# A decoder trunk on one core: the first pair of up blocks fed with unnormalised h, the reciprocal root and shift applied to its result

## The chip, the cores and the metric

One core of one Trainium2 chip runs the whole program in one launch. The metric is the device time in microseconds (us), the median of several executions. A profile is one further execution, recorded by the hardware profiler; its times are counted from the start of its span.

## What is computed

Four layers, each a token mixer (short convolution, RWKV-7, gated linear attention, short convolution) and then a gated convolutional FFN. There are 512 prompt tokens and 8 sample tokens, D = 1024 and 2816 hidden columns. The part that the change touches is the normalisation between the mixer and the FFN, and the first two hidden tiles:

```python
h = h + gt_m * rmsnorm(out, p['norm_g'][l, 1])
u = rmsnorm(h, p['norm_g'][l, 2]) * (1 + sc_f) + sh_f
# conv_ffn:
h_gate, h_val = jnp.split(x @ w_up, 2, axis=-1)
hc, new_buf = causal_dwconv(h_gate, buf, conv_w)
out = (jax.nn.silu(hc + conv_b) * h_val) @ w_down
```

`rmsnorm(x, g)` is `x * rsqrt(mean(x*x) + eps) * g`, with the mean over the 1024 columns of a token. sc_f, sh_f and gt_m come from the conditioning vector, one set for the prompt and one for each sample token. The root is one number for each token, so (h * a * r + s) @ W equals r * ((h * a) @ W) + s @ W, where a is the gain times (1 + sc_f), r the reciprocal root and s the shift.

## The kernel before

**Layout.** Activations lie transposed: 128 columns on the partitions, k = 0..7 tiles, and T = 520 tokens along the free axis (512 prompt, then 8 samples). h, proj (the output of the previous GEMM), u_hi and u_lo have this form. A GEMM operand is split into a high part, rounded to fp32r, and the low remainder.

**Blocks.** A block is one 128-column output of a GEMM. For each weight block SyncE loads w_raw (two slots, by parity), ScalarE rounds it to w_hi (`high`, 128x1024), GpSimd writes w_raw - w_hi to w_lo (`low`; `low_parts` does the same in four pieces of 128x256), and TensorE runs three products, hi x hi, lo x hi and hi x lo, each in two halves of 260 tokens: 48 matmuls of 260 columns. A load waits until the low part of the block two before it is done (`load_block`). The up GEMM has 22 hidden tiles of two blocks each, the gate block (even, PSUM pair 0) and the value block (odd, PSUM pair 1).

**Norms.** After the last block of "out" comes the plan's step "post": sums of squares of proj over the tokens (`token_sums`, TensorE), square root (`root`, ScalarE), reciprocal (`inverse_root`, VectorE), a spread of the reciprocal over all partitions into PSUM (`spread_rstd`, TensorE), and then on VectorE for each tile k a multiplication of proj by it (`times_rstd`) and the update of h. Then comes "pre" for the FFN: ScalarE squares each tile of h, TensorE sums, root, reciprocal and spread follow again, VectorE writes h times the reciprocal to `normed`, ScalarE makes u_hi and the unrounded u (`usb`) from it with scale and shift, and VectorE makes u_lo. TensorE's `gemm_pair` starts with the first tile of u: it runs blocks n0 and n0+1 tile by tile, 12 matmuls for each k, as the tiles come.

**Fill.** In layers 0 to 2 TensorE also does in the two norms the 16 modulation products of the next half layer (`ada_ahead`, four matmuls for each of them), in fixed places: four before post's spread, four behind it, four between the sums of pre, four behind pre's spread. Layer 3 has none. Every engine runs its instructions in the order written; the waits on semaphores are written by hand.

**Start of up.** For each hidden tile ScalarE copies the state columns (`place_state`) and the gate block into `gate`, frees PSUM pair 0, and rounds the next tile's first weight block; VectorE runs a convolution of three steps (`conv3`); ScalarE applies Silu and rounds the next tile's second weight block; VectorE multiplies by the value block (`times_tile`, which frees PSUM pair 1) and splits the product (`split_hidden`). TensorE transposes the tile's last rows (`turn_tail`) and the next state (`turn_state`) between tiles.

## Time and profile before

| | |
|---|---|
| runs | 3015.1, 3015.58 and 3020.77 us, median 3015.58 us |
| span of the profiled execution | 3014.3 us |
| TensorE matmuls | 2876.1 us, 95% of the span |
| VectorE | 1528.4 us, 51% |
| GpSimd | 1321.5 us, 44% |
| ScalarE | 1085.0 us, 36% |
| all that TensorE sat idle for ScalarE's squares (L1717 <- L1011) | 25.2 us |
| chain that ended last, TensorE's share | 62% |

The profiled execution stands 1.3 us under the median of the runs. Engines are PE = TensorE, DVE = VectorE, ACT = ScalarE, POOL = GpSimd, SP = SyncE. In a timeline, a row gives start, duration, engine, line of the kernel, operation, operands and count; what ended an idle time before it stands in brackets. A timeline row of two or more instructions has the time from the first's start to the last's end; an fp32 matmul counts as two records, an fp32r one as one.

### The profile page before, as it was taken

What the parts mean: (1) busy time and instruction counts of PE and PEld (TensorE: products, weight loads), DVE (VectorE), ACT (ScalarE), POOL (GpSimd) and SP (SyncE); (2) the same over time, 40 slices, a digit from 0 to 9 for tenths busy, and PEclk for the clock granted to TensorE, in tenths of its full rate; (3) what the DMA queues carried; (4) which work ended last, traced back from release to release, by engine and by line L of the source; (5) the groups of instructions that cost most, each with busy time, mean ns of one, the idle gap of its engine ahead of it and who ended that gap; (6) DMA issues with size and microseconds to landing.
All of it is one profiled execution on the core that took longest, in us unless ns stands there. A gap on an engine that the chain in (4) does not pass through costs nothing.

```text
span 3014.3 us, 72962 instructions
## 1 busy us (share of the span) xinstructions
PE 2876.1 (95%) x29617; PEld 2733.3 (91%) x29617; DVE 1528.4 (51%) x2080; ACT 1085.0 (36%) x2139; POOL 1321.5 (44%) x959
## 2 busy tenths in 40 slices
PE   6999999998989999999998999999999999899998
PEld 5998999997978877899997899889999899799998
DVE  3435666118357874666603242476650444566612
ACT  4224333225455652433323444343332422433322
POOL 3443444442435554344443273434444344344443
PEclk9999999999999999999999999999999999899999
DMA  7544333544411013333354323533334543133332
GB/s 269 164 151 159 95 92 88 158 128 136 119 44 32 4 37 124 120 89 92 99 159 152 99 64 112 169 123 89 92 116 146 173 120 91 57 92 92 91 91 85
DMA packets 465618, 332.56 MB, mean 110 GB/s; under 512 B 19914, under 2 KB 435608, under 8 KB 465122
## 3 DMA queue, kind: packets, MB, share of 16 engines
q1 hardware_dynamic: 461400, 325.24, 35.1%
q10 hardware_dynamic: 4010, 4.22, 0.6%
q8 instruction: 172, 2.82, 0.4%
q14 instruction: 36, 0.29, 0.0%
HBM read 319.62 MB, written 10.20 MB: 109 GB/s over the span
## 4 chain that ended last, share of the span: by engine, by line
PE 62%; DVE 4%; ACT 2%; issue 1%; DMA 1%; SPq 0%; POOL 0%; ACTq 0%; DVEq 0%
PE banks L1667 33%; PE banks L1675 16%; PE banks L2126 5%; PE banks L2133 1%; PE banks L1628 1%; PE banks L1973 1%; DVE h L2662 1%; PE banks L1690 1%; DVE proj L2606 1%; PE banks L1761 0%; DMA s_state<-in_state_wkv_b_dram 0%; ACT conv L1080 0%; PE banks L2135 0%; ACT uv L1433 0%; DVE proj_b L2606 0%
## 5 line engine op out<-in xcount | busy, mean ns | idle before, releaser
L765 POOL TENSOR_TENSOR w_lo<-w_raw,w_hi 128x1024 fp32r<-128x1024 f32 x395 | 1007.5, 2551 | 1108.1 <-ACT w_hi L981 1088.0
L1667 PE MATMUL banks<-u_hi,w_hi 128*128 128x260 f32 x4064 | 834.5, 287 | 14.2 <-ACT w_hi L981 9.4
L1667 PE MATMUL banks<-u_lo,w_hi 128*128 128x260 f32 x4064 | 825.1, 284 | 0.0
L1667 PEld LDWEIGHTS banks<-u_hi,w_hi 128*128 128x128 f32 x4064 | 627.4, 189 | 27.1 <-issue 15.2
L1667 PEld LDWEIGHTS banks<-u_lo,w_hi 128*128 128x128 f32 x4064 | 629.9, 189 | 1.6
L981 ACT ACTIVATE w_hi<-w_raw 128x1024 fp32r<-128x1024 f32 x402 | 424.5, 1056 | 454.2 <-PE banks L1675 284.4
L1675 PE MATMUL banks<-u_hi,w_lo 128*128 128x260 f32 x4064 | 527.5, 282 | 0.0
L1675 PEld LDWEIGHTS banks<-u_hi,w_lo 128*128 128x128 f32 x4064 | 502.1, 187 | 1.3
L1667 PE MATMUL banks<-hid_hi,w_hi 128*128 128x260 f32 x1664 | 336.3, 283 | 0.0
L1667 PE MATMUL banks<-hid_lo,w_hi 128*128 128x260 f32 x1664 | 335.2, 283 | 0.0
L3113 DVE TENSOR_TENSOR csb<-proj 128x520 f32 (+1 forms) x42 | 30.3, 722 | 470.8 <-ACT proj L1048 470.8
L2594 DVE TENSOR_TENSOR hid_lo<-prod,hid_hi 128x520 f32 x104 | 259.7, 2497 | 12.8
L1667 PEld LDWEIGHTS banks<-hid_hi,w_hi 128*128 128x128 f32 x1664 | 256.8, 188 | 5.0 <-issue 3.7
L2578 DVE SCALAR_TENSOR_TENSOR conv<-gate,vecs,conv 128x536 f32<-128x536 f32 x104 | 249.2, 2396 | 15.1 <-DVE conv L2576 0.8
L1667 PEld LDWEIGHTS banks<-hid_lo,w_hi 128*128 128x128 f32 x1664 | 256.1, 188 | 0.0
L1675 PE MATMUL banks<-hid_hi,w_lo 128*128 128x260 f32 x1664 | 217.0, 282 | 0.0
L1675 PEld LDWEIGHTS banks<-hid_hi,w_lo 128*128 128x128 f32 x1664 | 206.4, 188 | 0.0
L780 POOL TENSOR_TENSOR tail<-gate,ones 128x2 f32<-128x2 f32 x104 | 28.0, 269 | 339.1 <-ACT gate L1536 339.1
L1543 ACT ACTIVATE conv<-conv,vecs 128x536 f32<-128x536 f32 x88 | 65.5, 744 | 287.5 <-DVE conv L2578 287.5
L2575 DVE TENSOR_SCALAR conv<-gate,vecs 128x536 f32<-128x536 f32 x104 | 55.9, 538 | 194.5 <-ACT gate L1536 190.5
L1534 ACT ACTIVATE gate<-banks 128x260 f32<-128x260 f32 x88 | 34.1, 387 | 256.2 <-PE banks L1675 254.8
L2576 DVE SCALAR_TENSOR_TENSOR conv<-gate,vecs,conv 128x536 f32<-128x536 f32 x104 | 108.1, 1039 | 15.2 <-DVE conv L2575 1.7
(463 smaller groups left out, 3898.8 us busy)
## 6 DMA issues: line engine op xcount, KB each, us to landing
w_raw<-in_ffn_w_up_dram SPq DMA_DIRECT2D x176, 512.0 KB, 3.7
ada_raw<-in_ada_w_dram SPq DMA_DIRECT2D x96, 512.0 KB, 4.7
w_raw<-in_ffn_w_down_dram SPq DMA_DIRECT2D x64, 448.0 KB, 3.7
w_raw<-in_sconv_w_in_dram SPq DMA_DIRECT2D x48, 512.0 KB, 5.2
ada_ahead<-in_ada_w_dram SPq DMA_DIRECT2D x36, 512.0 KB, 7.7
ada_ahead_down<-in_ada_w_dram SPq DMA_DIRECT2D x36, 512.0 KB, 6.2
w_raw<-in_ffn_w_down_dram SPq DMA_DIRECT2D x32, 512.0 KB, 4.0
ada_pro<-in_ada_w_dram SPq DMA_DIRECT2D x6, 2048.0 KB, 21.2
```

The costliest lines, as they stand in the source:

```text
L765: pool.tensor_tensor(w_lo[:, s, :, :], w_raw[:, s, :, :], w_hi[:, s, :, :].bitcast(F32), ALU.subtract).then_inc(lo_done, 1)
L981: act.activation(w_hi[:, s, :, :], w_raw[:, s, :, :], ACT.Copy).then_inc(hi_done, 1)
L1534: act.activation(gate[:, e, 2:2 + HALF], tile_ps[0][0][:, 0:HALF], ACT.Copy)
L1543: act.activation(conv[:, e, 0:CWD], conv[:, e, 0:CWD], ACT.Silu, bias=vec("ffn_conv_b", l * FT + m)).then_inc(silu_done, 1)
L1667: pe.matmul(tile_ps[slot][half][0:width, 0:HALF], w_hi[:, s, k, 0:width], x[:, k0 + k, half * HALF:(half + 1) * HALF], start=start and k = ...
L1675: mm = pe.matmul(tile_ps[slot][half][0:width, 0:HALF], w_lo[:, s, k, 0:width], xh[:, k0 + k, half * HALF:(half + 1) * HALF], start=False, ...
L2126: mm = pe.matmul(out(rs), left(rs), right(rs), start=start, stop=stop)
L2575: link(dve.tensor_scalar(conv[:, e, 0:CWD], gate[:, e, 0:CWD], w[0], None, ALU.mult))
L2576: link(dve.scalar_tensor_tensor(conv[:, e, 0:CWD], gate[:, e, 1:1 + CWD], w[1], conv[:, e, 0:CWD], ALU.mult, ALU.add))
L2578: dve.scalar_tensor_tensor(conv[:, e, 0:CWD], gate[:, e, 2:2 + CWD], w[2], conv[:, e, 0:CWD], ALU.mult, ALU.add).then_inc(conv_done, 1)
L2594: dve.tensor_tensor(lo, prod[:, e, :], hi.bitcast(F32), ALU.subtract).then_inc(hid_ready, 1)
L3113: return dve.tensor_tensor(csb[:, 1, :], o, o, ALU.mult)
```

## The change

In all four layers the norm in front of the FFN (`defer=True` in the plan) is rearranged.

- **Post.** Eight `ada_ahead` products stand before the spread instead of four, and none behind it. VectorE first splits the shift of the FFN's modulation into `shift_parts`; after the samples' update of h it makes the samples' part of u_hi and u_lo from h times (1 + sc_f) times gain. TensorE runs `shift_products`, 32 matmuls of 18 columns, the shift times blocks n0 and n0+1. For each k, VectorE updates h, ScalarE makes u_hi as h times the scale, with no reciprocal root and no shift, and squares h, and VectorE makes u_lo from h two tiles later. TensorE runs the first `gemm_pair` on it, with the sums of squares between its matmuls.
- **Which tiles.** That first pair is hidden tile 1 (blocks loaded in the order tile 1, tile 0). Its result is copied to `early`, multiplied by the spread reciprocal root, and the shift product is added. Hidden tile 0 is the second pair; it runs on the normalised u as before, with weights in the new buffers `first_hi` and `first_lo`. Of these GpSimd makes one low half in four pieces (`low_first`) and VectorE the other.
- **Start of up.** The first three iterations are written out in a new order; hidden tile 2's first weight block is rounded ahead of tile 0's gate copy, and tile 1's Silu stands ahead of tile 2's gate copy on ScalarE.
- Some semaphores are merged (`side_loaded`), and one of the ahead buffers is elsewhere in memory.

```diff
+            def low_first(n):
+                pool.wait_ge(hi_done, n + 1)
+                for k in range(0, KT, 2):
+                    ins = pool.tensor_tensor(first_lo[:, 0, k:k + 2, :], w_raw[:, 0, k:k + 2, :],
+                                             first_hi[:, 0, k:k + 2, :].bitcast(F32), ALU.subtract)
+                ins.then_inc(lo_done, 1)
...
+                    if p["defer"]:
+                        for k in range(KT):
+                            act.wait_ge(h_ready, KT * p["post"] + k + 1)
...
+                            act.activation(u_hi[:, k, 0:TP], h[:, k, 0:TP], ACT.Copy, scale=p["mod"][:, KT + k, 0:1])\
+                               .then_inc(uhi_done, 1)
+                            act.wait_ge(sq_used, KT * i + k - 1)
+                            act.activation(sq[:, k % 2, :], h[:, k, :], ACT.Square).then_inc(sq_done, 1)
+                            if k == 3:
+                                high_first(n0 + 3, 1)
+                        act.wait_ge(sq_used, KT * (i + 1))
+                        root()
+                        act.wait_ge(block_done, n0 + 4)
+                        for s in range(2):
+                            act.activation(early[:, s, 0:HALF], tile_ps[s][0][:, 0:HALF], ACT.Copy)
...
+            def shift_products(n, t0, l):
+                pe.wait_ge(parts_ready, l + 1)
...
+                    for k in range(KT):
+                        for w in (w_hi, w_lo):
+                            pe.matmul(tile_ps[s][1][:, SHIFT_COLS], w[:, s, k, :], shift_parts[:, k, :],
+                                      start=(k == 0 and w is w_hi), stop=(k == KT - 1 and w is w_lo))
...
+                    before = KT if p["defer"] else KT // 2
                     if in_norms(p["half"]):
-                        for i in range(KT // 2):
+                        for i in range(before):
                             ada_ahead(p["half"], i)
                     spread_rstd(p["norm"])
+                    if p["defer"]:
+                        shift_products(n0, t0, l)
...
+                    first_pair()
+                    hidden_tile(1, 0, False, second_state, (q0 + 1, 1))
+                    hidden_tile(1, 1, True, lambda: turn_tail(q0 + 2, 0))
```

On TensorE, in layer 0 from the last sums of proj (L1717 before, L1832 in the change) on. Before:

```order
L1717 MATMUL banks<-csb,ones 32x136 x8
L1628 MATMUL banks<-ada_ahead_0_177,cT 32x256 x4
...
L1759 MATMUL banks<-rstd,ident 128x8
L1761 MATMUL banks<-rstd,ident 128x128 x4
L1628 MATMUL banks<-ada_ahead_4_181,cT 32x256 x4
...
L1717 MATMUL banks<-csb,ones 32x136 x12
```

In the change:

```order
L1729 MATMUL banks<-ada_ahead_5_189,cT 32x256 x4
L1729 MATMUL banks<-ada_raw,cT 32x256 x8
L1874 MATMUL banks<-rstd,ident 128x8
L1876 MATMUL banks<-rstd,ident 128x128 x4
L1814 MATMUL banks<-shift_parts,w_hi 128x18
L1814 MATMUL banks<-shift_parts,w_lo 128x18
...
L1722 MATMUL banks<-ident,acc_sb 128x36 x2
L1791 MATMUL banks<-u_hi,w_hi 128x260 x2
L1791 MATMUL banks<-u_hi,w_lo 128x260 x2
```

The spread moved behind all eight products, and between it and the first pair stand 32 shift matmuls.

On VectorE, in layer 0's post, from the samples' update of h on. Before:

```order
L2654 TENSOR_TENSOR h<-h,s_76 128x8x8
L2606 TENSOR_TENSOR proj<-proj,banks 128x512 x2
L2662 SCALAR_TENSOR_TENSOR h<-proj,mod_m,h 128x512
L2606 TENSOR_TENSOR proj<-proj,banks 128x512
L2662 SCALAR_TENSOR_TENSOR h<-proj,mod_m,h 128x512
```

In the change:

```order
L2810 TENSOR_TENSOR h<-h,s_76 128x8x8
L2815 TENSOR_TENSOR s_76<-h,mod_f 128x64
L2816 CAST u_hi<-s_76 128x8x8
L2817 TENSOR_TENSOR u_lo<-s_76,u_hi 128x8x8
L2753 TENSOR_TENSOR proj<-proj,banks 128x512 x2
L2826 SCALAR_TENSOR_TENSOR h<-proj,mod_m,h 128x512
L2753 TENSOR_TENSOR proj<-proj,banks 128x512
L2826 SCALAR_TENSOR_TENSOR h<-proj,mod_m,h 128x512
L2831 SCALAR_TENSOR_TENSOR u_lo<-h,mod_f,u_hi 128x512
```

Three instructions came in ahead of the first tile, and a third one, u_lo, into each tile's turn.

On ScalarE, at the start of up in layer 0, from the table load on. Before:

```order
L1524 ACT_TABLE_LOAD
...
L986 ACTIVATE gate<-banks 128x8x2
...
L1536 ACTIVATE gate<-banks 128x8
...
L981 ACTIVATE w_hi<-w_raw 128x1024
...
L1543 ACTIVATE conv<-conv,vecs 128x536
```

In the change:

```order
L1021 ACTIVATE w_hi<-w_raw 128x1024
L1026 ACTIVATE gate<-banks 128x8x2
...
L1600 ACTIVATE conv<-conv,vecs 128x536
L1021 ACTIVATE w_hi<-w_raw 128x1024
L1619 ACTIVATE gate<-early,shift_out_cols 128x512
L1620 ACTIVATE gate<-early 128x8
...
L1600 ACTIVATE conv<-conv,vecs 128x536
L1026 ACTIVATE gate<-banks 128x8x2
L1626 ACTIVATE gate<-banks 128x260
L1627 ACTIVATE gate<-banks 128x252
L1628 ACTIVATE gate<-banks 128x8
L1010 ACTIVATE w_hi<-w_raw 128x1024
```

A weight rounding moved ahead of the first gate copy, and a second Silu (L1600) stands ahead of the copy of tile 2's gate block.

## Rows read from the trace of the kernel before

**Rows 1.** The page's head and its part on engines: busy us (share), instructions.

```profile
span 3014.3 us, 72962 instructions
PE 2876.1 (95%) x29617; PEld 2733.3 (91%) x29617; DVE 1528.4 (51%) x2080; ACT 1085.0 (36%) x2139; POOL 1321.5 (44%) x959
```

**Rows 2.** Waits of PE: us in total, times, longest.

```profile
PE banks L1717 <- ACT csb L1011: 25.2, 35, 2.8
```

**Rows 3.** Busy by stretch: us, PE, PEld, DVE, ACT, POOL, PE's granted clock, DMA.

```profile
292.00:296.00 4.00, 3.85 (x19) 3.88 (x20) 2.94 (x3) 0.79 (x3) 2.43 (x1) 0.57 0.07 18
312.00:323.50 11.50, 11.50 (x99) 11.48 (x98) 7.91 (x8) 3.65 (x9) 5.72 (x4) 1.00 0.33 95
2590.00:2605.70 15.70, 8.14 (x75) 3.95 (x76) 11.29 (x22) 6.56 (x11) 0.00 (x0) 0.50 0.11 32
```

**Rows 4.** Timeline of PE in layer 0's two norms and first pair.

```profile
257.57 0.44 PE L1717 MATMUL banks<-csb,ones 128*32 128x136 f32 x8 [0.45 <-ACT csb L1042]
257.83 1.91 PE L1628 MATMUL banks<-ada_ahead,cT 128*32 128x256 f32 x32
259.67 0.39 PE L1759 MATMUL banks<-rstd,ident 128*128 128x8 f32 x2
...
274.36 0.39 PE L1759 MATMUL banks<-rstd,ident 128*128 128x8 f32 x2 [1.54 <-DVE rstd L2552]
...
277.69 0.48 PE L1690 MATMUL banks<-u_hi,w_hi 128*128 128x260 f32 x2
...
289.09 0.65 PE L1696 MATMUL banks<-u_lo,w_hi 128*128 128x260 f32 x4
```

**Rows 5.** Timeline of DVE in layer 0's norms; the last row, layer 3's post.

```profile
261.16 1.28 DVE L2606 TENSOR_TENSOR proj<-proj,banks 128x512 f32<-128x512 f32 x2 [0.19 <-PE banks L1761]
262.36 0.75 DVE L2662 SCALAR_TENSOR_TENSOR h<-proj,mod_m,h 128x512 f32<-128x512 f32 x1
263.02 0.68 DVE L2606 TENSOR_TENSOR proj<-proj,banks 128x512 f32<-128x512 f32 x1
263.62 0.75 DVE L2662 SCALAR_TENSOR_TENSOR h<-proj,mod_m,h 128x512 f32<-128x512 f32 x1
...
269.92 1.40 DVE L2662 SCALAR_TENSOR_TENSOR h<-proj,mod_m,h 128x512 f32<-128x512 f32 x2
...
276.69 0.22 DVE L2627 TENSOR_TENSOR s<-s,mod_f 128x64 f32<-128x64 f32 x1
276.95 0.20 DVE L2636 CAST u_hi<-s 128x64 fp32r<-128x64 f32 x1
...
2588.20 1.29 DVE L2606 TENSOR_TENSOR proj<-proj,banks 128x512 f32<-128x512 f32 x2 [0.95 <-PE banks L1761]
```

**Rows 6.** Timeline of ACT in layer 0's norms.

```profile
270.70 1.30 ACT L1011 ACTIVATE csb<-h 128x520 f32<-128x520 f32 x2 [0.62 <-DVE h L2662]
...
276.56 0.82 ACT L1078 ACTIVATE u_hi<-prod,mod_f 128x512 fp32r<-128x512 f32 x1 [3.29 <-DVE prod L2606]
```

**Rows 7.** Line L2363, small matmuls on new weights: ns min/median/max, first to last start.

```profile
L2363 PE MATMUL banks<-rw_r,bonus_ones x16: 256/256/277, 1138.3 to 1140.0; 128*128 128x8 f32 x16
```

**Rows 8.** Timeline of ACT at the start of up, layer 0.

```profile
295.22 0.74 ACT L1543 ACTIVATE conv<-conv,vecs 128x536 f32<-128x536 f32 x1 [3.21 <-DVE conv L2578]
295.87 1.04 ACT L981 ACTIVATE w_hi<-w_raw 128x1024 fp32r<-128x1024 f32 x1
```

**Rows 9.** Timeline of DVE at the start of up, layer 0.

```profile
292.43 2.65 DVE L2578 SCALAR_TENSOR_TENSOR conv<-gate,vecs,conv 128x536 f32<-128x536 f32 x1 [0.15 <-DVE conv L2576]
```

**Rows 10.** Timeline of POOL at the start of up, layer 0.

```profile
292.08 2.43 POOL L765 TENSOR_TENSOR w_lo<-w_raw,w_hi 128x1024 fp32r<-128x1024 f32 x1 [0.68 <-ACT w_hi L981]
```

**Rows 11.** Timeline of PE: heads of block n0+6 in layers 0 and 3, end of layer 3's pair.

```profile
316.94 0.27 PE L1710 MATMUL banks<-ident,tail 128*10 128x128 f32 x1
...
2618.80 0.64 PE L1696 MATMUL banks<-u_lo,w_hi 128*128 128x260 f32 x4
...
2644.69 0.27 PE L1710 MATMUL banks<-ident,tail 128*10 128x128 f32 x1
```

More of the change, by code:

```diff
@@ L419, in trunk_kernel @@
             mixer = l % 3
-            norm("pre", l, mod=mod_m, group=2 * l, pre=pre, post=post, full=mixer == 1, half=2 * l + 1)
+            norm("pre", l, mod=mod_m, group=2 * l, pre=pre, post=post, full=mixer == 1, half=2 * l + 1, defer=False)
             count["split"] += 1
+            count["us"] += 1
             pre += 1
@@ L1677, in gemm, with gemm_pair @@
                 return mm.then_inc(block_done, 1)
-            def gemm_pair(n, pre, xh, xl, ready, hi=(uhi_done, None), weights=(w_hi, w_lo), start=True, stop=True):
+            def gemm_pair(n, pre, xh, xl, ready, hi=(uhi_done, None), weights=(w_hi, w_lo), start=True, stop=True,
+                          behind=None):
                 pe.wait_ge(hi_done, n + 2)
```

276 lines of the change are left out of this document (205 added, 71 removed).

## The prediction

> **What bounds the kernel now.** I read the page first: TensorE has matmuls in flight for 95% of the span [rows 1]. In the stretch of the up GEMM it is busy for all of 11.5 us of 11.5, at the full granted clock [rows 3]; nothing can be won there except by taking matmuls away, and the change takes none away. So the question is what TensorE does when it isn't full. The view of its waits names the norms: idle for the squares of h, 25.2 us in all [rows 2]. Then I read the timelines of the four FFN norms. In layer 0 the last sums of proj start at 257.57 and the first pair of up at 277.69 [rows 4]; of these 20 us TensorE owes only the sums, the spreads and, in layers 0 to 2, the sixteen modulation products.
>
> All times below are of the one profiled execution (span 3014.3 us), which stands 1.3 us under the median of the runs. I give each layer's sum as the time at which the head of block n0+6 is reached, since behind it both kernels run the same steady tiles. "End of the pair" is the start of the last four matmuls of the normalised pair plus 0.5.
>
> **What it wins.** After the change the same head is reached with two blocks fewer behind the normalised pair, since one whole pair was done during the update of h. A block of 48 matmuls takes 11.5 / 2 = 5.75 us [rows 3], so 11.5 us a layer.
>
> **What the update of h loses, layer 0.** The step that sets the pace there is VectorE's turn for each tile.
> - Start: eight modulation products stand before the spread now. Four take 259.67 - 257.83 = 1.84 us [rows 4], so the spread is issued at 261.5 instead of 259.7. Behind the samples' update come three more linked small instructions at 0.26 each [rows 5]. The first multiplication of proj starts at 263.9 instead of 261.16 [rows 5]: 2.7 later. VectorE's split of the shift (two small instructions before the reciprocal, 0.5 us) is hidden behind the eight products.
> - Turn: multiplication 0.60, update 0.66 (263.62 - 263.02 and 263.02 - 262.36, [rows 5]). The new u_lo is an instruction of the update's form, so I give it 0.66: 1.92 us a tile instead of 1.26. The last tile of h was ready at 269.92 + 1.40 = 271.3 [rows 5]; six u_lo come before its update now, so 4.0 later on top of 2.7: 278.0.
> - ScalarE does a u_hi (0.72 apart, 0.82 long) and a square (0.65) for each tile [rows 6], 1.37 us, and one weight rounding of 1.04 [rows 8]: within 1.92, no loss.
> - TensorE: 12 matmuls at 5.75 / 48 = 0.12 and four sums, 257.83 - 257.57 = 0.26 [rows 4]: 1.70 a tile, also within 1.92, but with little to spare.
> - Shift products: no row shows fp32r matmuls of 18 columns. The nearest are small ones that each load new 128x128 weights: 16 records in 1140.0 - 1138.3 us, 0.113 each [rows 7]. 32 of them are 3.6 us; at half the clock they would be 7.2, and if weights hid entirely, nearly 0. I take 3.6. In layers 0 to 2 they run from 263.0 to 266.6, and the first u_hi is ready at 266.2: hidden but for 0.7, which TensorE's spare time takes up.
> - Tail: before, the spread of pre was issued 3.0 us after the last h (274.36 - 271.3, [rows 4]). Now the last square waits behind a u_hi, the sums behind eight matmuls, and the spread behind the last u_lo products and four modulation products: 278.0 + 0.8 + 0.65 + about 1.1 for the matmuls ahead and the sums = 280.6, then 0.5 for the rest of the pair and 1.84 for the products: 283.0. That is 5.0, so 1.9 more.
>
> Together the normalised pair starts and ends 2.7 + 4.0 + 1.9 = 8.6 us later in layer 0; layers 1 and 2 have the same form, and with 0.2 for POOL's passes I take **8.8 for each of the three**.
>
> **Start of up.** Here I find a new wait. Before, the head of n0+6 came 316.94 - 289.09 = 27.85 us after the start of the pair's last matmuls [rows 4, 11]: two stretches of 11.7 for a tile with its transposes, 2.6 for the first gate copy, and 1.75 because the granted clock lay at 1.2 GHz for 3.5 us [rows 3]. Layer 1 has the same pattern, layer 2 has no fall of the clock and 26.3.
> After the change ScalarE rounds a weight block (1.04) before the gate copy. Gate copies end 2.1 after the pair's end, TensorE starts block n0+4 at 2.5, as before. VectorE's three steps of tile 0 start 2.2 after the end and finish at 6.8: one of them waits for POOL's low part, like the 2.65 us one, which ends only behind the POOL row that started at 292.08 [rows 9, 10]. Silu of tile 0 starts at 6.8. From this Silu VectorE needs 0.8 for Silu, 1.5 for products and cast and 2.7 for the low half (again behind POOL), then 2.4 for the three steps of tile 1: 7.4. Only then does ScalarE run the second Silu, and only behind that come tile 2's gate copy and the rounding for n0+6 (0.7 + 1.0 + 1.05). So w_hi of n0+6 is there at 6.8 + 7.4 + 2.8 = 17.0. TensorE was ready for it at 8.6 + 5.75 + 0.2 = 14.5. **TensorE idles 2.5 us there.** The head comes 17.5 after the start of the last matmuls. Queued behind it: the whole stream of up.
>
> Layer 0: 27.85 - 17.5 - 8.8 = 1.55 won. Layer 1 the same. Layer 2: 26.3 - 17.5 - 8.8 = 0.
>
> **Layer 3** has no modulation products to fill or delay. The multiplication starts at 2588.20 [rows 5] plus 0.5 for the shift's split; h is done 14.1 later, at 2602.8. But TensorE's granted clock was 0.50 over the whole stretch to 2605.7 [rows 3]. I assume it rises by 2593 under the new load: shift products from 2588.6 to about 2594, eight tiles of 1.70, pair done at 2608, sums at 2607.5. TensorE sets the pace here. Spread at 2609.6, pair 3.4 later and 11.4 to its last matmuls at full clock (289.09 - 277.69, [rows 4]): 2624.5 instead of 2618.80 [rows 11], 5.7 later. No copy of modulation sums stands before the table load, so the start of up is 1.4 shorter: 16.1 instead of 17.5, against 2644.69 - 2618.80 = 25.9 [rows 11]. Won: 25.9 - 16.1 - 5.7 = 4.1.
>
> **Sum:** 1.55 + 1.55 + 0 + 4.1 = 7.2 us won. The clock: a gap of 2.5 us before up cost 1.75 in two of four layers. A fall in the first gap is swallowed by the new wait, a fall after the new wait is not; and layer 3's gaps may bring one too. I take one such fall in all and a little, 2 us. So 3014.3 - 5.2 = 3009.1 for the execution, and with 1.3 for the median **3010.5 us**. Between 3006 and 3015 I call it the same case: unknowns are the shift products (0 to 7.2 us a layer, of which some 2 can be hidden) and one or two falls of the clock.
>
> **Rivals.**
> 1. *The new wait isn't there, or the clock stays up.* If POOL's pass misses one of VectorE's steps (2.0 us each), the second Silu comes 2 us earlier in each layer, and with no fall of the clock nothing of the 2 is paid: 3010.5 - 8 - 2 = 3000. For it: POOL and VectorE met in only one of three steps before. Against: the low part starts just as the second step does.
> 2. *VectorE loses the turns to POOL (slower).* The place is post. Before, POOL's four pieces ended when the first update began; now four more pieces (`low_first`, together 2.8) run through the first turns, and every update and u_lo reads two operands from SBUF. The row shows what such a meeting costs: a step that takes 0.78 undisturbed took 2.65, to 0.6 behind POOL's end [rows 9, 10]. I counted 0.2 for it. If the pieces hold VectorE for all of 2.8 and tile 1's steps meet POOL once more (2.0), it is 4.6 a layer, 18 in all: 3010.5 + 18 = 3028. It decides against the change from 2.8 a layer on. For it: the forms are the same. Against: pieces of 0.7 let VectorE in between, and TensorE has 1 us of spare in these turns.
> The Trainium skill has a rule that speaks for this rival: by "SBUF — State Buffer", section "SBUF: two separate sides", the port pair that VectorE and GpSimd share is an exclusive lock, and a VectorE operation with two SBUF inputs fully blocks while a GpSimd operation holds it. By that rule the trace agrees for whole passes; whether pieces let VectorE in at once no row here shows.
> 3. *The clock falls oftener.* In layer 3 it lay at half for 15.7 us with TensorE half busy [rows 3]. If each layer pays 1.75 after the new wait, and layer 3's normalised pair runs its first 5 us at half clock (2.5), it is 9.5 instead of 2: 3018.
> 4. *It doesn't do what it says.* If the first pair can't run beside the update, because its shift products or its sums hold it, the pair lands behind the update and the gain is gone: about 3015 to 3017.
>
> **How the numbers follow.** Forecast 0.56, rival 1 0.18, rival 2 0.10, rival 3 0.10, rival 4 0.06. A measurement of this kernel can tell about 0.2%, 6 us, from no change, so faster means under 3009.5. A little under half of the forecast's case lies there: 0.24 + 0.18 = 0.42. Slower is rival 2 and a part of rival 3: 0.13. Same is the rest, 0.45. The range 3000 to 3020 leaves out the far half of rival 1, most of rival 2 and the end of rival 3, about 2 in 10.
>
> **What the changed profile would show.** Right: VectorE's turn in post of 1.9 us, TensorE busy with u_hi matmuls in it, the normalised pair of layer 0 starting near 286.3; on TensorE an idle time of 2 to 3 us before block n0+6, ended by ScalarE's w_hi; idle for squares near zero. Wrong: turns of 2.5 us or updates of 1.4 (rival 2), a granted clock near 0.5 behind the start of up in three or four layers (rival 3), or no idle time before n0+6 (rival 1). I would be most wrong if the order on ScalarE let tile 2's gate copy come sooner than VectorE's six steps allow.

## The result

| | us |
|---|---|
| the changed kernel, four runs | 3033.26 to 3037.41, median 3034.18 |
| the kernel before, with the runs beside it | 3015.1 to 3020.77, median 3017.87 |
| ratio, 95% interval | 1.0054 (1.004 to 1.0068) |
| span of the profiled execution, before and after | 3014.3 and 3035.7 |

The change makes the kernel 16 us slower. The forecast was 3010.5 with a range to 3020: wrong in sign. The profiled execution of the changed kernel is the slowest of its four, 3 us above their median, so the 21.4 us between the two spans hold a few that the medians do not; where those lie is shown below. The ratios below leave out one execution, of the experiment e9_all_wide, that took 9.7 ms where its other five took 3004.05 to 3009.26 us; no run here says why.

The head of the page after, to be read beside [rows 1]: busy us (share), instructions.

```profile
span 3035.7 us, 72983 instructions
PE 2909.2 (96%) x29745; PEld 2762.7 (91%) x29745; DVE 1564.1 (52%) x2156; ACT 1108.6 (37%) x2191; POOL 1312.5 (43%) x967
```

TensorE is busy for 33 us more. Nothing had been taken off it, and that is the first sign of where the time is.

**The waits of TensorE** after, beside [rows 2] (us in total, times, longest):

```profile
PE banks L1768 <- ACT w_hi L1010: 14.3, 12, 4.2
...
PE banks L1832 <- ACT csb L1051: 10.7, 16, 1.1
```

The idle time for the squares, 25.2 us before, is 10.7: the change did remove the wait that it went for. It is no contradiction that the kernel got slower. The work that took the place of the idle time is longer than the idle time was.

**By stage.** Two landmarks are in both kernels: the root of the norm "post" (ScalarE, L1002 before, L1042 after) and the last four matmuls of the normalised pair ([rows 4, 11] for layers 0 and 3). Two rows of after for layer 0, from the timelines of ACT and of PE:

```profile
258.03 0.38 ACT L1042 ACTIVATE std<-banks,eps_col 128x136 f32<-128x136 f32 x1
```

```profile
302.35 0.65 PE L1799 MATMUL banks<-u_lo,first_hi 128*128 128x260 f32 x4
```

| us | layer 0 | layer 1 | layer 2 | layer 3 |
|---|---|---|---|---|
| root of post to last matmuls of the normalised pair, before | 31.01 | 30.75 | 31.60 | 34.44 |
| the same, after | 44.32 | 44.31 | 45.82 | 46.46 |
| later by | 13.31 | 13.56 | 14.22 | 12.02 |
| predicted | 8.8 | 8.8 | 8.8 | 5.7 |
| from there to the next root of post, before | 383.61 | 383.59 | 382.09 | 376.07 |
| the same, after | 373.22 | 373.20 | 373.23 | 366.35 |
| shorter by | 10.39 | 10.39 | 8.86 | 9.72 |
| predicted | 10.35 | 10.35 | 8.8 | 9.8 |

The gain was predicted to 0.1 us in each layer. The price was too small by 4.5 to 6.3 us in each layer, 21.0 in all. The four layers together lose 13.75 us. Of the rest of the 21.4, 6.5 us lie in layer 1's RWKV mixer, which the change to the norms doesn't touch (root of pre to root of the next post: 524.86 before, 531.35 after), and 1.2 in all other stages.

**TensorE in the rearranged norm.** Busy time by stretch of layer 0 (from:to, us, PE busy and its records, PE's granted clock, DMA share, GB/s): first of the kernel before, then of the changed one.

```profile
257.50:277.70 20.20, 15.39 (x226) 0.92 0.74 261
```

```profile
257.50:268.00 10.50, 10.48 (x119) 0.85 0.53 178
268.00:285.70 17.70, 17.70 (x161) 0.90 0.47 182
285.70:290.90 5.20, 5.20 (x77) 1.00 0.00 2
```

Before, TensorE had 4.8 us of idle time between the sums of proj and the first pair of up. A pair of 11.5 us was put into it. After the change there is none left: 33.38 us of 33.4. From the first u_hi on it is TensorE, not VectorE, that sets the pace (the next rows show it), which the prediction had excluded.

**One tile of the first pair**, timeline of PE after (start, us, matmuls): tile 4 of layer 0 and the head of tile 5.

```profile
275.68 0.40 PE L1791 MATMUL banks<-u_hi,w_hi 128*128 128x260 f32 x2
...
276.72 0.44 PE L1832 MATMUL banks<-csb,ones 128*32 128x136 f32 x8
277.09 0.74 PE L1799 MATMUL banks<-u_lo,w_hi 128*128 128x260 f32 x4
277.66 0.41 PE L1791 MATMUL banks<-u_hi,w_hi 128*128 128x260 f32 x2
```

From 275.68 to 277.66 the tile takes 1.98 us; I had 1.70. Eight matmuls 1.04 to the start of the sums (0.96 expected), sums 0.37 (0.26), four matmuls 0.57 (0.48). The sums and their neighbours on both sides each cost 0.1 more than their like in an unbroken run.

TensorE waits for nobody in these tiles. The u_hi of tile 5, timeline of ACT:

```profile
274.72 0.71 ACT L1102 ACTIVATE u_hi<-h,mod_f 128x512 fp32r<-128x512 f32 x1
```

It is ready at 275.43, 2.2 us before its matmuls start (277.66). The tile's square is ready at 275.95 and its sums start at 278.71; VectorE's u_lo is ready at 276.21 and is used at 279.08.

**The granted clock.** Timeline of PE after at the end of the shift products and the pair's start:

```profile
264.60 0.26 PE L1814 MATMUL banks<-shift_parts,w_lo 128*128 128x18 f32 x1
264.71 0.26 PE L1814 MATMUL banks<-shift_parts,w_hi 128*128 128x18 f32 x1
...
265.23 0.36 PE L1814 MATMUL banks<-shift_parts,w_lo 128*128 128x18 f32 x1
265.44 0.36 PE L1814 MATMUL banks<-shift_parts,w_hi 128*128 128x18 f32 x1
...
268.00 0.78 PE L1791 MATMUL banks<-u_hi,w_hi 128*128 128x260 f32 x2
...
271.65 0.43 PE L1791 MATMUL banks<-u_hi,w_hi 128*128 128x260 f32 x2
```

The shift products start 0.111 us apart, as estimated, and from 264.9 on 0.213 apart: the clock went from 2.4 to 1.2 GHz, and the pair's first tile, still at that level, took 3.65 us. By stretch, ahead of the pair and the pair, in all four layers:

```profile
262.40:268.00 5.60, 5.60 (x40) 0.72 0.80 276
268.00:285.70 17.70, 17.70 (x161) 0.90 0.47 182
1228.00:1233.60 5.60, 5.60 (x41) 0.75 0.76 257
1233.60:1251.50 17.90, 17.90 (x162) 0.89 0.46 185
1976.50:1982.10 5.60, 5.60 (x37) 0.67 0.87 291
1982.10:2001.00 18.90, 18.90 (x162) 0.83 0.41 166
2606.40:2614.70 8.30, 7.15 (x36) 0.50 0.22 65
2614.70:2633.10 18.40, 18.40 (x161) 0.85 0.00 1
```

Length times clock is 15.9, 15.9, 15.7 and 15.6: the pair is always 8 x 1.98 us of work, and what differs between the layers is only how long the lower level lasted. Before the change the clock fell in layer 0's norms too (0.92 above), but the pair came behind that and took 11.4 us to its last matmuls ([rows 4], 277.69 to 289.09). Only in layer 3 did a fall reach into the pair before the change: the level of 1.2 GHz lasted to 2610.2, and the pair took 13.1 us to its last matmuls (2605.71 to 2618.80).

So two theories for the 21 us: **A**, TensorE's own work, the dearer tile (0.28 x 8 = 2.2 us a layer) and half clock inside the pair (1.8 to 3.2 us); **B**, the chain through ScalarE, whose square waits for a free slot in every tile (idle 0.74 before L1105), so that u_hi, the root and everything behind come late. The start of up was in question as well: I had named a new wait there.

### The profile page after: what moved, and what is told of

It reads as the page before. It is cut to its first block, busy times and chain, and to the rows that moved or that the text cites. A ratio compares the mean times of both kernels' runs of the same rounds, so it can differ in the third digit from the quotient of the medians.

```text
span 3035.7 us, 72983 instructions
## 1 busy us (share of the span) xinstructions
PE 2909.2 (96%) x29745; PEld 2762.7 (91%) x29745; DVE 1564.1 (52%) x2156; ACT 1108.6 (37%) x2191; POOL 1312.5 (43%) x967
## 4 chain that ended last, share of the span: by engine, by line
PE 62%; DVE 4%; ACT 3%; issue 1%; POOL 0%; DVEq 0%; ACTq 0%
PE banks L1768 31%; PE banks L1776 16%; PE banks L2262 5%; PE banks L1791 1%; PE banks L1729 1%; PE banks L2269 1%; PE banks L2109 1%; PE banks L1799 1%; PE banks L1814 1%; PE banks L1832 1%; ACT conv L1140 0%; DVE conv L2723 0%; DVE proj L2753 0%; PE banks L2271 0%; DVE conv L2722 0%
## 5 line engine op out<-in xcount | busy, mean ns | idle before, releaser
L780 POOL TENSOR_TENSOR w_lo<-w_raw,w_hi 128x1024 fp32r<-128x1024 f32 x387 | 986.6, 2550 | 1102.5 <-ACT w_hi L1010 1069.6
L1768 PE MATMUL banks<-u_hi,w_hi 128*128 128x260 f32 x3936 | 809.3, 287 | 20.3 <-ACT w_hi L1010 14.3
L1768 PE MATMUL banks<-u_lo,w_hi 128*128 128x260 f32 x3936 | 799.6, 284 | 0.0
L1768 PEld LDWEIGHTS banks<-u_hi,w_hi 128*128 128x128 f32 x3936 | 608.0, 190 | 35.0 <-issue 18.3
L1768 PEld LDWEIGHTS banks<-u_lo,w_hi 128*128 128x128 f32 x3936 | 610.6, 189 | 1.6
L1010 ACT ACTIVATE w_hi<-w_raw 128x1024 fp32r<-128x1024 f32 x386 | 407.6, 1057 | 450.6 <-PE banks L1776 291.6
L1776 PE MATMUL banks<-u_hi,w_lo 128*128 128x260 f32 x3936 | 511.8, 282 | 0.0
L1776 PEld LDWEIGHTS banks<-u_hi,w_lo 128*128 128x128 f32 x3936 | 486.3, 187 | 1.7
L2741 DVE TENSOR_TENSOR hid_lo<-prod,hid_hi 128x520 f32 (+1 forms) x104 | 252.3, 2426 | 12.1
L2725 DVE SCALAR_TENSOR_TENSOR conv<-gate,vecs,conv 128x536 f32<-128x536 f32 x104 | 224.2, 2156 | 14.2 <-DVE conv L2723 0.9
L1600 ACT ACTIVATE conv<-conv,vecs 128x536 f32<-128x536 f32 x88 | 65.5, 744 | 305.1 <-DVE conv L2725 305.1
L2723 DVE SCALAR_TENSOR_TENSOR conv<-gate,vecs,conv 128x536 f32<-128x536 f32 x104 | 120.2, 1156 | 15.7 <-DVE conv L2722 4.6
```

Of the source, the lines that this page charges most:

```text
L780: pool.tensor_tensor(w_lo[:, s, :, :], w_raw[:, s, :, :], w_hi[:, s, :, :].bitcast(F32), ALU.subtract).then_inc(lo_done, 1)
L1010: act.activation(w_hi[:, s, :, :], w_raw[:, s, :, :], ACT.Copy).then_inc(hi_done, 1)
L1600: act.activation(conv[:, e, 0:CWD], conv[:, e, 0:CWD], ACT.Silu, bias=vec("ffn_conv_b", l * FT + m)).then_inc(silu_done, 1)
L1768: pe.matmul(tile_ps[slot][half][0:width, 0:HALF], w_hi[:, s, k, 0:width], x[:, k0 + k, half * HALF:(half + 1) * HALF], start=start and k = ...
L1776: mm = pe.matmul(tile_ps[slot][half][0:width, 0:HALF], w_lo[:, s, k, 0:width], xh[:, k0 + k, half * HALF:(half + 1) * HALF], start=False, ...
L2723: link(dve.scalar_tensor_tensor(conv[:, e, 0:CWD], gate[:, e, 1:1 + CWD], w[1], conv[:, e, 0:CWD], ALU.mult, ALU.add))
```

## The experiments

All ratios are to the kernel before, run on the same chip in the same rounds. 0.001 is 3 us. The changed kernel had rounds of its own (and so had e1 to e4, e5 to e8, and e9 to e11), so a gain over the changed kernel is a difference of two ratios and is good to about 0.0017, 5 us.

| run | ratio | 95% interval |
|---|---|---|
| the change | 1.0054 | 1.004 to 1.0068 |
| e1_no_shift | 1.002 | 1.0011 to 1.003 |
| e2_silu_later | 1.0042 | 1.0025 to 1.0059 |
| e3_sums_paired | 1.0017 | 1.0008 to 1.0027 |
| e4_before_swap | 0.9985 | 0.9976 to 0.9995 |
| e5_wide_shift | 1.002 | 1.001 to 1.003 |
| e6_table_later | 1.0034 | 1.0021 to 1.0047 |
| e7_early_root | 1.0001 | 0.9991 to 1.001 |
| e8_all | 0.9991 | 0.9981 to 1.0001 |
| e9_all_wide | 0.9956 | 0.9943 to 0.9968 |
| e10_wide_paired | 1.0001 | 0.9992 to 1.001 |
| e11_after_swap | 1.0039 | 1.0024 to 1.0053 |

### e1: without most of the shift products

```diff
-                    for k in range(KT):
-                        for w in (w_hi, w_lo):
-                            pe.matmul(tile_ps[s][1][:, SHIFT_COLS], w[:, s, k, :], shift_parts[:, k, :],
+                    pe.matmul(tile_ps[s][1][:, SHIFT_COLS], w_hi[:, s, 0, :], shift_parts[:, 0, :],
```

> The changed kernel with 2 instead of 32 shift products in each of the four norms (the shift's part of hidden tile 1 is left out). Theory A, TensorE's own work fills the rearranged norm (in layer 0 it is busy for 33.4 us of the 33.4 from the sums of proj to the normalised pair): the 30 products take 30 x 0.111 = 3.3 us at the full clock, 4.4 as they ran in layer 0. But the first u_hi is ready at 266.9 and the first pair started at 268.0, so the start moves by at most 1.1 us; if the granted clock is full for the first tile of the pair as well (3.65 us before, 2.0 for a later tile), another 1.6. In all 1.1 to 2.7 us a layer, 4 to 11 us. Theory B, ScalarE's squares set the pace from the first tile on and the shift products are cover only: 0 to 1 us a layer, at most 4 in all, with tile 0 of the pair still at 3.6 us.

It gains 10 us by ratio, the upper end of theory A, but not where A had put it. From the root of post to the root of pre the four layers take 26.90, 26.82, 24.87 and 24.84 us, against 27.19, 27.18, 28.68 and 29.20 with the products. Timeline of PE, layer 0:

```profile
267.77 0.56 PE L1791 MATMUL banks<-u_hi,w_hi 128*128 128x260 f32 x1 [3.79 <-ACT u_hi L1102]
```

and by stretch the first pair in layers 0 and 3:

```profile
267.70:286.10 18.40, 18.32 (x160) 0.86 0.49 194
...
2607.40:2625.00 17.60, 17.60 (x160) 0.90 0.01 1
```

In layers 0 and 1 TensorE now idles 3.8 us for the first u_hi, so there the products were mostly hidden, as I had predicted: in layer 0 the pair starts 9.1 us behind the root instead of 10.0. The clock falls all the same, with TensorE idle in place of narrow products, the pair runs at 0.86 instead of 0.90, and of the 0.9 us only 0.3 is left. The pair is still 8 x 1.98. In layers 2 and 3 the products themselves had run at 1.2 GHz (0.67 and 0.50 above) and had held up the pair: it starts 7.8 and 7.7 us behind the root instead of 10.3 and 11.3.

### e3: the sums of two tiles together, room for four squares

```diff
-                            act.wait_ge(sq_used, KT * i + k - 1)
-                            act.activation(sq[:, k % 2, :], h[:, k, :], ACT.Square).then_inc(sq_done, 1)
+                            act.wait_ge(sq_used, KT * i + k - 3)
+                            act.activation(four_squares(k), h[:, k, :], ACT.Square).then_inc(sq_done, 1)
...
+                            if k % 2:
+                                for j in (k - 1, k):
+                                    pe.wait_ge(sq_done, KT * i + j + 1)
+                                    token_sums(four_squares(j), j == 0, j == KT - 1).then_inc(sq_used, 1)
```

> The changed kernel with room for four squares (two more in the buffer early) and the sums of two tiles together behind every second tile. Theory A, TensorE is the bound of the first pair and each change from matmuls of u to the sums and back costs it time (a tile takes 1.99 us, of which 12 x 0.12 = 1.44 are matmuls, 0.26 was expected for the sums, 0.3 is neither): two tiles take 3.99 - 0.3 = 3.7 us, 0.3 x 4 = 1.2 us a layer, some 4 us in all, and the waits of ScalarE for the sums (0.74 each) are gone without effect of their own. Theory B, ScalarE's wait for the square's slot holds up u_hi and so TensorE: the tile falls to VectorE's 1.92 us, 0.5 us a layer, 2 us in all. Either way ScalarE's squares end ahead of 281.

The pair by stretch, four layers:

```profile
269.90:286.30 16.40, 16.40 (x162) 0.90 0.48 194
1235.40:1252.00 16.60, 16.60 (x162) 0.88 0.49 194
1980.10:1996.40 16.30, 16.30 (x162) 0.90 0.60 228
2610.50:2627.30 16.80, 16.80 (x161) 0.87 0.00 1
```

Length times clock is now 14.6 to 14.8, 1.1 us less a layer with the same matmuls: four of the eight changes from u's matmuls to the sums and back are gone, 0.28 us for each. Two tiles take 3.67 us (275.21 to 278.88), theory A's 3.7. A tile without sums takes 1.44 us (275.21 to 276.65) and one with the sums of two 2.23: what is above 12 x 0.12 and 2 x 0.26 is paid once for two tiles. Theory B is out: operands of the changed kernel lie ready 2 us ahead (above), and a pair that VectorE paced could not run under 1.92 a tile. The ratio gives 11 us, more than these 4 x 1.1; the layers take 25.95, 25.95, 24.36 and 27.51 from root to root, 8.5 us less together, and layer 2 has in this execution 4.3 us less because its clock lay low for less time. Run e10 below separates the two.

### e5: the same shift products, 252 columns wide

The 18 columns are read 14 times over. The result is the same, 14-fold.

```diff
-                            pe.matmul(tile_ps[s][1][:, SHIFT_COLS], w[:, s, k, :], shift_parts[:, k, :],
+                            pe.matmul(tile_ps[s][1][:, HALF:HALF + WIDE * 2 * NSEQ], w[:, s, k, :],
+                                      shift_parts[:, k, :].unsqueeze(1).to_broadcast([P, WIDE, 2 * NSEQ]),
```

> The changed kernel with each shift product made 252 columns wide (the same 18 columns 14 times over) instead of 18. At the full clock a product of 18 columns took 0.111 us and one of 260 takes 0.12, so the same result costs 32 x 0.009 = 0.3 us more a layer. Theory A, the granted clock falls ahead of the first pair because TensorE streams few columns there, whatever its instructions: the half-clock time within the first pair (3.7, 4.0, 6.5 and 5.4 us in the four layers of the changed kernel's profile) falls to 0 to 3.4 us, and the pair's 17.7, 17.8, 18.8 and 18.4 us to 16 to 17.6: 0 to 10 us in all, most in layers 2 and 3. Theory B, the fall follows from what stands before the shift products (sums, modulation products, waits) and its length doesn't depend on them: same half-clock times, 0 to +2 us.

By stretch, the products of layer 0 and then the first pair in all layers:

```profile
262.00:266.90 4.90, 4.90 (x41) 1.00 0.74 239
266.90:283.00 16.10, 16.10 (x162) 1.00 0.56 223
1226.70:1242.80 16.10, 16.10 (x161) 1.00 0.55 220
1972.40:1988.50 16.10, 16.10 (x162) 1.00 0.56 220
2601.00:2617.00 16.00, 16.00 (x162) 1.00 0.00 2
```

More work on TensorE, and 10 us less by ratio. The granted clock was 1.00 in all four pairs, 0.83 to 0.90 before this edit, and from root to root the layers take 2.45, 2.45, 3.99 and 3.11 us less. The wide products start 0.13 us apart. In layer 3 the pair still starts 10.6 us behind the root (11.3 before the edit), so there part of the low stretch is left. That is theory A for the clock, and it isn't merely that narrow products are slow: e1 had none of them and the pair still started at 1.2 GHz.

How much of this could be one execution differing from another? Three other runs leave the norm as the changed kernel has it (e2, e6 and e11). From root to root their four layers take 109.3, 112.0 and 109.3 us together, the changed kernel's 112.3, and e5's 100.3. So the length of the low stretch varies by up to 3 us between executions, and e5's gain is 9 us over the best of the four. In all three, the narrow products of layer 1 ran at a granted clock of 1.00 and the fall came within the pair instead (0.90, 17.7 us).

### e10: both

> The changed kernel with the sums of two tiles together and the wide shift products, nothing else. If the tile's cost and the clock are independent terms of TensorE's time, the first pair takes 8 x 1.82 = 14.6 us in every layer, and the ratio to the kernel before is 1.0054 - 0.0037 - 0.0034 = 0.998 to 0.999. If with less work on TensorE VectorE's turn of 1.92 us becomes the bound, the pair takes 15.4 or more and the ratio is 1.0 or above.

```profile
267.90:283.20 15.30, 15.30 (x161) 1.00 0.59 238
1225.00:1240.40 15.40, 15.40 (x162) 1.00 0.59 231
1969.20:1984.30 15.10, 15.10 (x162) 1.00 0.57 221
2598.00:2612.70 14.70, 14.70 (x162) 1.00 0.01 2
```

Between the two expectations. Only layer 3 has the 14.7 that e3's work asks for. In layer 0 the matmuls of u_lo of every second tile start at 271.19, 275.04, 278.88 and 282.54: two tiles take 3.85, 3.84 and 3.66 us, the first two of them twice VectorE's turn of 1.92. The u_lo matmuls of tiles 1, 3 and 5 start at 268.96, 272.81 and 276.66, each 0.05 or 0.06 us after VectorE has finished that u_lo (268.91, 272.75, 276.60). Now that TensorE has room, the bound that I had predicted from the start does appear, and the two gains, 11 and 10 us, don't add up but give 16. Such a wait stands in no idle time, since matmuls are in flight over it: TensorE reads busy for 15.30 of 15.30 us. With the clock at 1.00 in both, the sums in pairs take 0.7 to 1.3 us a layer off e5's pairs, 3.8 in all; what e3's ratio showed beyond that is the clock and the error of a difference of ratios.

### e2: tile 1's Silu behind tile 2's gate copy

```diff
                         send_rows(0, 0)
-                        silu(q0 + 1, 1, 1)
...
                         if second:
+                            silu(q0 + 1, 1, 1)
                             send_rows(0, 1)
```

> The changed kernel with tile 1's Silu behind tile 2's gate copy and the rounding of block n0+6 on ScalarE. Theory A, the new wait at the start of up is real and is that order's: TensorE's idle for w_hi (L1010) falls from 14.3 us to under 10 us, 2 to 2.5 us a layer, 6 to 10 us in all. Rival, the tiles' chain on VectorE (three convolution steps, product, split) is late anyway: the wait reappears on the value block's PSUM or at the Silu, under 2 us in all.

The ratio says 1.0042 with an interval that holds 1.0054; from the root of pre to the next root of post layer 0 takes 390.38 us, against 390.35. Timeline of PE, idle times from block n0+6 on, the changed kernel and then this one:

```profile
319.16 0.48 PE L1768 MATMUL banks<-u_hi,w_hi 128*128 128x260 f32 x2 [0.48 <-ACT w_hi L1010]
325.65 0.48 PE L1768 MATMUL banks<-u_hi,w_hi 128*128 128x260 f32 x2 [0.40 <-ACT w_hi L1010]
```

```profile
326.87 0.48 PE L1768 MATMUL banks<-u_hi,w_hi 128*128 128x260 f32 x2 [1.11 <-ACT w_hi L1010]
```

The wait at n0+6 is gone and one block later there is a longer one, 1.11 us where the two waits before were 0.48 and 0.40: the rival. The new wait that I had priced at 2.5 us was only 0.48 in this execution, because the clock had fallen behind the pair and TensorE reached the block later. The prediction had said that a fall there is swallowed by the wait.

### e6: the Silu table behind the first gate copy

```diff
                 elif p["kind"] == "up":
-                    act.activation(warm[:, :], eps_col[:, :], ACT.Silu)
...
                         take_gate(q0, 0)
+                        act.activation(warm[:, :], eps_col[:, :], ACT.Silu)
```

> The changed kernel with ScalarE's switch to Silu (a table load of 1.28 us at 301.75 in layer 0) behind the first gate copy instead of ahead of the rounding of block n0+4. Theory A, TensorE's idle of 1.42 us behind the normalised pair is this load: the idle goes, 1.3 us a layer, 5 us in all. Rival, what TensorE gains it gives back at block n0+6 or n0+7, because VectorE's chain of the first tiles is what is late: under 1.5 us in all.

The idle time of 1.42 us behind the normalised pair is gone. On PE, block n0+6 of layer 0:

```profile
318.43 0.48 PE L1767 MATMUL banks<-u_hi,w_hi 128*128 128x260 f32 x2 [1.54 <-ACT w_hi L1010]
```

The wait for w_hi of n0+6 is 1.54 instead of 0.48, but that is the clock: at the start of up it fell in layer 0 of the changed kernel and not here. In layer 2 it fell in neither, and there the wait is 1.54 in both. So nothing is given back at n0+6: its w_hi is ready 15.6 us behind the start of the pair's last matmuls in layer 2, instead of 16.7, because the first gate copy comes 1.4 us earlier. From the root of pre to the next root of post layers 0 to 2 are 1.04 to 1.06 us shorter and layer 3 is 0.1 shorter, 3.3 in all; the ratios differ by 6 us, with intervals that overlap at their ends. By the profile that is theory A in the three layers that had the idle time (layer 3 had none), a little under its 1.3. With e2 it shows that at the start of up the chain from the first gate copy over VectorE's first tiles to w_hi of n0+6 is what is late, as the prediction had it: what starts the chain earlier is won, what TensorE alone wins or loses ahead of it is not.

### e7, e8 and e9: towards a better kernel

e7 is e3 with these edits:

```diff
+                            if k == KT - 1:
+                                spread_rstd(p["norm"])
+                            if k in (1, 3, 5, 6):
+                                for j in ((k, k + 1) if k == 6 else (k - 1, k)):
...
                         gemm_pair(n0 + 2, p["us"], u_hi, u_lo, (u_ready, KT * (p["split"] - 1)), weights=(first_hi, first_lo))
+                        if in_norms(2 * l + 2):
+                            for i in range(KT + 4, 2 * KT):
+                                ada_ahead(2 * l + 2, i)
```

> The kernel of paired sums with three more edits: the sums of squares 6 and 7 stand ahead of the last tile's matmuls, so that root, reciprocal and spread run beside it (spread before its last four matmuls); four of the eight modulation products between the pairs go behind the normalised pair; their sums are copied by ScalarE behind the first gate copy. Theory A, TensorE's work is the bound and it has idle left only behind the normalised pair (1.42 + 0.27 + 0.48 us in layer 0) and, in layer 3, between the pairs: the normalised pair starts 3.0 us behind the first pair's end instead of 5.2, the four products (1.93 us) fill the idle behind it: 1.5 us a layer in layers 0 to 2 and 2 in layer 3, 6 us in all under the kernel of paired sums. Theory B, between the pairs it is the chain root, reciprocal, spread, normalisation, rounding: the same 2.2 us earlier start, but the products behind the pair delay block n0+4 by their full 1.93: 2 us in all.

Timeline of PE, from the end of the first pair to the normalised one:

```profile
285.60 0.72 PE L1804 MATMUL banks<-u_lo,w_hi 128*128 128x260 f32 x4
286.25 1.93 PE L1734 MATMUL banks<-ada_ahead,cT 128*32 128x256 f32 x32
...
288.70 0.48 PE L1796 MATMUL banks<-u_hi,first_hi 128*128 128x260 f32 x2 [0.26 <-DVE u_lo L2794]
```

The normalised pair starts 2.4 us behind the first one's end instead of 5.1, and by ratio it is 5 us better than e3: nearer to theory A's 6 than to B's 2, though the two intervals touch.

> All together on the changed kernel: paired sums, early root with four products behind the normalised pair, the Silu table behind the first gate copy, and the swap in the RWKV output stage. If the gains add up (paired sums 8 to 11 us by ratio 1.0054 to 1.0017, early root 2 to 6, table 1 to 5, swap 3 to 6) it stands 14 to 28 us under the changed kernel, 2 us above to 12 under the kernel before. If VectorE's chain at the start of up gives back what comes earlier, it is level with the kernel before (within 3 us).

e8 adds e6's edit and the swap of e4: 0.9991, inside the expected 2 above to 12 below, at its upper part. It is also within 3 us of the kernel before, so it doesn't decide between the two expectations.

> The kernel of all edits together (ratio 0.9991 to the kernel before) with the shift products made 252 columns wide as well. Theory A, the first pair then runs wholly at the full clock in every layer: its 18.25, 17.65, 17.53 and 17.99 us lose half of their 5.0, 3.6, 3.3 and 4.3 us at half the clock, less 0.3 a layer for the wider products, 1.4 to 2.2 us a layer, 6 to 8 us in all, ratio 0.9965 to 0.997. Theory B, with the sums in pairs and the root early the light stretch falls elsewhere (between the pairs, at the start of up) and the half clock with it: under 2 us in all, ratio 0.9985 or above.

e9 adds the wide products: 0.9956. Against e8 (other rounds) it is 10 us by ratio and 9.2 from root to root in the profiles, theory A and a little more, and it beats the kernel before by 13 us (10 to 17). All four first pairs run at a granted clock of 1.00.

### e4 and e11: the RWKV output stage

```diff
                     shifted(1)
+                    scaled(2)
                     gate_tile(0, 1)
                     for k in range(2, KT):
-                        scaled(k)
                         shifted(k)
+                        if k + 1 < KT:
+                            scaled(k + 1)
                         gate_tile(k - 1, 1)
```

> The kernel before with one swap in the RWKV output stage: VectorE does the addition of the shift (L3057, operands all in SBUF) right behind the gate multiplication and the scaling with a PSUM operand after it. In the profiles this addition takes 0.75 us or 1.87 us by whether it meets GpSimd's u_lo, 3 of 8 slow before and 7 of 8 after the change, which is 4.4 us of the difference of the two spans. Theory A, it is that meeting: all eight are at 0.75 to 1.0, and the time is 2 to 5 us under the kernel before, with less spread between executions. Theory B, the long ones are something else (the chain of proj's columns, the granted clock): the same count of long ones, no change.

The line of the addition before (ns min/median/max), then of e4:

```profile
L3057 DVE SCALAR_TENSOR_TENSOR rw_kk<-rw_kk,vecs,rw_v x8: 746/752/1866, 1142.9 to 1160.0; 128x512 f32<-128x512 f32 x8
```

```profile
L3057 DVE SCALAR_TENSOR_TENSOR rw_kk<-rw_kk,vecs,rw_v x8: 744/745/747, 1142.5 to 1158.2; 128x512 f32<-128x512 f32 x8
```

(The expectation counted three of eight slow before and seven after; the rows say two and six.) None of the eight is slow now, and the kernel before gains 4.5 us (1.5 to 7). It is the meeting with GpSimd, and the swap ends it.

> The changed kernel with the swap in the RWKV output stage alone. Theory A, the swap and the change to the norms don't touch each other: all eight additions of the shift take 0.75 us, and against the changed kernel it wins what the kernel before won (ratio 1.0054 - 0.0015) or up to 0.001 more, since the changed kernel's profile had six slow ones and the one before two: 1.003 to 1.004. Theory B, most of the 16 us that the change lost are this collision: ratio 1.001 or below.

1.0039, all eight at 0.74 to 0.75: theory A. The collision is independent of the norms. Both kernels lose by it about alike (0.0015 each), so it explains why one profile stood far above the other, but next to nothing of the ratio 1.0054.

## Why the prediction was wrong, point by point

- **VectorE's turn**: right. Turns of 1.92 us (h at 268.65 and 270.58), first multiplication at 264.27 (263.9 predicted). The last h starts at 278.05 and is ready at 278.8 (278.0 predicted): 0.4 from the later start, and 0.4 from one turn of 2.31 in which u_lo waited for a u_hi behind ScalarE's rounding of a weight block.
- **POOL's pieces in post** (rival 2): they cost 0.4 us where 0.2 was counted. The samples' three small instructions took 0.65, 0.62 and 0.68 us under them instead of 0.26 each, and the turns of 1.92 show nothing of them; but the pieces had ended at 264.95, before the first such turn, so what rival 2 feared in the turns wasn't put to the test.
- **Shift products**: 3.6 predicted, 4.67 measured in layer 0 because the clock fell in their midst. That they are hidden but for 0.7 holds in layers 0 and 1 (e1: the pair starts 0.9 and 0.7 earlier without them). In layers 2 and 3 it fails, 2.5 and 3.6 us, again by the clock.
- **"TensorE 1.70, within 1.92"**: this is the step that failed. The tile was summed from matmuls in an unbroken run (0.12) and from the sums as they lay elsewhere (0.26). Interleaved it is 1.98 (e3: 1.83 with half the changes). And since the pair starts 1.0 us behind the first u_hi (ready at 266.96) with a first tile of 3.65, a turn longer than VectorE's 1.92 can never make that good. The prediction wasn't at one with itself here either: 1.92 - 1.70 leaves 0.22 us a tile, and rival 2 counted on 1 us of TensorE's spare time in the same turns. With this term and the next one taken away (e10), the last matmuls of the normalised pair come 10.0, 10.3, 9.9 and 6.8 us later than before, against 8.8, 8.8, 8.8 and 5.7 predicted: 16 of the 21 us by which the price was too small are these two terms.
- **The clock**: mis-sized, and put in the wrong place. I had looked at falls at the start of up and taken 2 us in all. It lay at 1.2 GHz inside the first pair in every layer, and cost 17.7 x 0.10, 17.9 x 0.11, 18.9 x 0.17 and 18.4 x 0.15 = 9.7 us there; e5 took it away and gained 12.0 us from root to root in its profile and 10 by ratio. The row that warned of it stood in front of me: the granted clock of layer 3's norm, 0.50 [rows 3]. Before, the low level met a TensorE that was half idle in the norms, and cost matmuls of a pair only in layer 3, 1.7 us. The change moved full work into the stretch where the clock was low.
- **The tail** (5.0 predicted): the last sums come at 284.71 instead of about 280, by 2.0 for the dearer tiles, 1.8 for the clock and 1.4 for the later start of the pair (268.0 instead of 266.6), less 0.7 that TensorE's path had in hand in the prediction. Behind them the chain is as predicted: 2.5 us from their end to the spread (2.4), 3.3 from there to the normalised pair.
- **Start of up**: right as a sum in all four layers (table), and in part by luck. The wait at n0+6 was 0.48 instead of 2.5 us in layer 0, where a fall of the clock came ahead of it and was swallowed, as predicted; in layer 2, with no fall, it was 1.54. The chain was overpriced: block n0+6 starts 16.8 us behind the last matmuls' start, not 17.5. What that wins is lost behind it, where layer 0 takes 0.8 longer than before to the next root, 0.4 of it a second wait for w_hi one block on that the prediction doesn't have.
- **Layer 3**: 5.7 predicted, 12.0 measured. The assumption that the clock rises by 2593 "under the new load" had no row behind it: it stayed low through the shift products and into the pair.
- **Rivals**: rival 4 named the right place (the pair held by its shift products and its sums) but stopped at "the gain is gone", 3017, at a chance of 0.06. Nothing in it says why the loss should stop there. Rival 3 had the clock falling oftener but behind the pair.

One sum would have told: TensorE's idle time in layer 0's norm is 20.2 - 15.4 = 4.8 us. That, and 2 us at the start of up, is about all that a rearrangement can win in a layer as long as the clock stays as it is. The change adds shift products (4.7 as they ran), the changes between kinds of matmul (2.2), and the clock (1.8), 8.7 us by this rough count. TensorE from one root of post to the next in layer 0, before and then after, measures it:

```profile
258.08:672.70 414.62, 407.43 (x3524) 0.99 0.38 115
```

```profile
258.03:675.57 417.54, 414.52 (x3556) 0.99 0.37 114
```

It is idle for 3.0 us instead of 7.2 and busy for 7.1 us more: 4.2 won, 7.1 paid, 2.9 lost (13.31 - 10.39). Over the four layers it is 16.2 won and 30.0 paid. I worked instead with the pair's 11.5 us as the gain and VectorE as the bound, and subtracted delays.

## What to carry to other kernels

Moving work into a gap wins at most the idle time of the engine that does the work, not the length of the work; read that idle time first, by stretch, and hold everything the move adds on that engine against it. If the gap lies where TensorE's granted clock is low, price the moved matmuls at that level, and look whether what stands ahead of them can be given a form under which the clock stays up, as 252 columns in place of 18 did here. A price for an instruction taken from an unbroken run of its kind doesn't hold between other kinds.

## What the runs showed of the hardware that I had not expected

**The clock and the width of a product.** 32 products of 18 columns, back to back with TensorE busy for all of 5.6 us, stood at granted clocks of 0.72, 0.75 and 0.67 in layers 0 to 2; with 252 columns each the same stretch of layer 0 stood at 1.00, and so did all twelve first pairs behind such products (e5, e9, e10). The fall doesn't come at a fixed place: in e2, e6 and e11 the narrow products of layer 1 stood at 1.00, and the clock fell behind them. A stretch that the profile shows as wholly busy can still lie at the lower level.

**VectorE and GpSimd, a coin toss.** The same two instructions of the RWKV stage, timelines of DVE and POOL before:

```profile
1151.83 0.75 DVE L3057 SCALAR_TENSOR_TENSOR rw_kk<-rw_kk,vecs,rw_v 128x512 f32<-128x512 f32 x1
```

```profile
1151.88 1.84 POOL L931 TENSOR_TENSOR u_lo<-gated_sb,u_hi 128x512 fp32r<-128x512 f32 x1 [1.89 <-ACT u_hi L1501]
```

and after:

```profile
1159.56 1.90 DVE L3226 SCALAR_TENSOR_TENSOR rw_kk<-rw_kk,vecs,rw_v 128x512 f32<-128x512 f32 x1
```

```profile
1159.61 1.30 POOL L956 TENSOR_TENSOR u_lo<-gated_sb,u_hi 128x512 fp32r<-128x512 f32 x1 [1.89 <-ACT u_hi L1565]
```

Both times the records start 0.05 us apart. Once GpSimd is the one held up (1.84 instead of 1.30) and VectorE isn't, once VectorE is (1.90 instead of 0.75), which costs its turn 1.1 us. Two of eight lost in the profile before, six in the one after, which is 4.4 of the 6.5 us of that stage. The seven other profiles with the old order have 5, 4, 5, 3, 3, 0 and 3 of eight (e1, e2, e3, e5, e6, e7, e10); the four with the swap (e4, e8, e9, e11) have none. The Trainium skill, page "SBUF — State Buffer", section "SBUF: two separate sides", says that of a VectorE operation with two SBUF inputs and a GpSimd operation that reads SBUF the one that starts first gets the shared port pair for the whole instruction and the other fully blocks. The trace agrees that one of them is held; which one, the recorded starts don't tell, since VectorE's is the earlier both times.
